# Experts' results scattered by rows to a table in DRAM and gathered per token, in place of a sorted buffer on the chip and a 0/1 matrix product

## The reference, cut to what matters

```python
oh_g = one_hot(top_k(x1 @ w_rg + b_rg, 1))            # group
le_sel = (x1 @ w_re + b_re)[group of the token]
e_val, e_idx = top_k(le_sel, 2)                        # two experts in it
comb = g_w * oh_g * (softmax(e_val) at e_idx)          # the two weights
y = sum over all 32 experts of ((silu(x1 @ w_gate) * (x1 @ w_up)) * comb) @ w_down
x2 = layer_norm(2 ** 0.25 * x1 + y)
gate = sigmoid(x2 @ w_ple_gate + b); x3 = layer_norm(2 ** 0.25 * x2 + gate * (p @ w_ple))
```

## Time and profile before

| what | us |
|---|---|
| median of three executions | 591.2 |
| span of the profiled execution | 587.8 |
| median less that span | 3.4 |
| TensorE busy in the span | 532.5 |
| VectorE busy | 291.9 |
| ScalarE busy | 193.0 |
| GpSimd busy | 58.6 |

### The profile page before, as it was taken

The page is one execution under the profiler, slowest core; times in us unless marked ns, Lnnn a source line. Parts: engine busy times, 40 slices in busy tenths (PEclk is TensorE's granted clock), DMA queues, the critical chain, the costliest instruction groups (busy, mean ns, idle before and its releaser), DMA issues.

```text
span 587.8 us, 9534 instructions
## 1 busy us (share of the span) xinstructions
PE 532.5 (91%) x3628; PEld 383.2 (65%) x3628; DVE 291.9 (50%) x621; ACT 193.0 (33%) x363; POOL 58.6 (10%) x86
## 2 busy tenths in 40 slices
PE   4999869999999979988999999998889899859992
PEld 3999768888999978756654545444444445346771
DVE  3442786565474865686722222312222222359976
ACT  4434443444462360163241111111111121345433
POOL 2000003322443420000000000000000000000121
PEclk9999999999999989979999999999999999969997
DMA  9995336865322940195739999999999999950001
GB/s 286 368 346 183 123 117 189 261 212 165 122 95 94 325 175 1 51 424 241 301 128 423 420 421 423 421 421 423 421 421 421 423 421 420 363 194 1 1 36 54
DMA packets 47563, 151.86 MB, mean 258 GB/s; under 512 B 3104, under 2 KB 27877, under 8 KB 35104
## 3 DMA queue, kind: packets, MB, share of 16 engines
q1 hardware_dynamic: 42754, 136.93, 60.2%
q0 software_dynamic: 3728, 12.08, 6.7%
q10 hardware_dynamic: 1046, 2.37, 1.2%
HBM read 148.59 MB, written 2.90 MB: 258 GB/s over the span
## 4 chain that ended last, share of the span: by engine, by line
PE 69%; DMA 12%; DVE 11%; ACT 4%; issue 3%; POOL 1%; SPq 0%; DVEq 0%; POOLq 0%; ACTq 0%
PE bank L1486 16%; PE bank L1805 15%; DMA ring<-in_w_up_dram 11%; PE bank L1454 8%; PE bank L1818 7%; PE bank L1674 5%; PE bank L1827 2%; PE bank L1904 2%; PE bank L1752 2%; PE bank L1432 1%; PE bank L1541 1%; ACT arena L630 1%; PE bank L1474 1%; PE bank L1811 1%; DMA arena<-in_x_prompt_dram 1%
## 5 line engine op out<-in xcount | busy, mean ns | idle before, releaser
L1805 PE MATMUL bank<-ring,arena 128*64 128x256 f32 x1024 | 128.9, 392 | 10.8 <-DMA ring<-in_w_up_dram 6.7
L1805 PEld LDWEIGHTS bank<-ring,arena 128*64 128x64 f32 x1024 | 70.9, 134 | 66.9 <-issue 27.5
L1243 DVE TENSOR_TENSOR arena<-bank,arena 128x512 f32 x32 | 22.1, 692 | 143.9 <-PE bank L1827 143.9
L1486 PE MATMUL bank<-x_high,w_high 128*128 128x320 f32 x248 | 79.1, 319 | 0.0
L1486 PE MATMUL bank<-x_low,w_high 128*128 128x320 f32 x248 | 76.6, 309 | 0.0
L1486 PE MATMUL bank<-x_high,w_low 128*128 128x320 f32 x248 | 76.4, 308 | 0.0
L1818 PE MATMUL bank<-ring,arena 128*64 128x512 f32 x256 | 61.9, 604 | 0.0
L895 DVE TENSOR_TENSOR w_low<-ring,w_high 128x1024 fp32r<-128x1024 f32 x32 | 40.0, 1258 | 29.7 <-ACT w_high L574 29.7
L1486 PEld LDWEIGHTS bank<-x_high,w_high 128*128 128x128 f32 x248 | 46.6, 188 | 1.4 <-issue 1.3
L1486 PEld LDWEIGHTS bank<-x_low,w_high 128*128 128x128 f32 x248 | 46.7, 188 | 0.1
L1486 PEld LDWEIGHTS bank<-x_high,w_low 128*128 128x128 f32 x248 | 46.5, 188 | 0.0
(11 more groups left out here) (301 smaller groups left out, 878.7 us busy)
## 6 DMA issues: line engine op xcount, KB each, us to landing
ring<-in_w_gate_dram SPq DMA_DIRECT2D x32, 1024.0 KB, 18.1
ring<-in_w_up_dram SPq DMA_DIRECT2D x32, 1024.0 KB, 20.1
ring<-in_w_down_dram SPq DMA_DIRECT2D x32, 1024.0 KB, 16.8
ring<-in_w_in_dram SPq DMA_DIRECT2D x16, 1024.0 KB, 10.2
arena<-in_cache_k_dram POOLq DMA_DIRECT2D x16, 256.0 KB, 4.4
arena<-in_cache_v_dram POOLq DMA_DIRECT2D x16, 256.0 KB, 3.2
ring<-in_w_o_dram SPq DMA_DIRECT2D x4, 1024.0 KB, 9.6
ring<-in_w_ple_gate_dram SPq DMA_DIRECT2D x4, 1024.0 KB, 15.6
```

The source lines that it names most:

```text
L1243: V.tensor_tensor(YsT[:, :, bass.ds(place, WIN)].rearrange("p (d c) n -> p c d n", d=2), b[:, :].rearrange("p (c d n) -> p c d n", c=4, d= ...
L1486: last = mm(bank[j % 2][:, 0:T], w[:, j % 4, k, :], x[:, k, :], start=(k == n == 0), stop=(k == KD - 1 and n == 2))
L1805: last = mm(b[WIN * f:WIN * (f + 1), 0:256].rearrange("p (s n) -> p s n", s=2), x[:, WIN * k:WIN * (k + 1)], w[:, :, k, f, :], start=(k == ...
```

## The change

The result of an expert is no longer turned and kept on the chip. ScalarE copies y into one of four `y_s` buffers in turn, and GpSimd issues an indirect DMA that writes its 128 rows of 512 numbers to `y_rows`, a table in DRAM of 1280 such rows, two for each pair, at row numbers that VectorE works out once (`result_rows`). Slots beyond the expert's count get a row number outside the table, and such rows are not written. When all 32 scatters have landed, GpSimd reads the flag, passes the loop for crowded experts and issues six indirect DMAs, which gather for each tile of tokens the first and the second row pair (4 KB a token) into `y_mine`. `combined` multiplies them by the token's two weights and adds them to x1, which VectorE has multiplied by 2 ** 0.25 after the first four experts. `turn_result`, `put`, `slot_weights`, `turn_pairs`, `pairs_out`, `turn_sorted` and `combine` go, with what belongs to them on ScalarE and VectorE. `high_gate` stands behind the last result now, all eight together; `low_gate` has four before and four after the first tile's norm. Loads of ln3 and the gate's bias wait for a semaphore that GpSimd raises once the gathers are issued. In `down`, TensorE now waits for ScalarE's copy of the result before.

```diff
@@ on-chip buffers
-        CT = at(69120, [P, PAIRS])
-        YsT = at(61440, [P, KD, SORTED])
+        y_s = [at(off, [P, 512]) for off in (69120, 71168, 73216, 85248)]
+        y_mine = at(38912, [P, 2 * TILES, D])
+        row_f = at(87296, [P, WINDOWS, 32])
-        x2 = at(61440, [P, TILES, D])
+        x2 = x1
+        y_rows = nc.dram_tensor("y_rows", (2 * PAIRS, 512), F32, kind="Internal").ap()
@@ GpSimd
+            def scatter(src, row, done):
+                pool.indirect_dma_start(y_rows, bass.IndirectOffsetOnAxis(ap=row, axis=0), src, None,
+                                        bounds_check=2 * PAIRS - 1, oob_is_err=False).then_inc(done, 16)
+            pool.wait_ge(rows_set, 1)
+            for n in range(EXPERTS):
+                pool.wait_ge(main["ys"], n + 1)
+                if n % 4 == 1 and n > 4:
+                    pool.wait_ge(y_out[3], 16 * (n // 4))
+                    pool.sem_inc(last_free, 1)
+                scatter(y_s[n % 4], row_i[:, 0, n:n + 1], y_out[n % 4])
+            for n in range(4):
+                pool.wait_ge(y_out[n], 16 * (EXPERTS // 4))
+            pool.wait_ge(starts_set, 1)
+            crowded = pool.value_load(flag[0:1, 0:1], min_val=0, max_val=1)
+            with pool.If(crowded > 0):
...
+            for t in ORDER:
+                r = ROWS[t]
+                for c in range(2):
+                    pool.indirect_dma_start(y_mine[0:r, 2 * t + c, :], None, y_rows.rearrange("(n d) f -> n (d f)", d=2),
+                                            bass.IndirectOffsetOnAxis(ap=mine_i[0:r, 3 * c + t:3 * c + t + 1], axis=0)).then_inc(y_here[t], 16)
+            pool.memset(scratch[:, 2:3], 0.0).then_inc(moe_done, 1)
@@ ScalarE
-            def result_out(q, n):
+            def result_out(q, n, b, free=None, turn=0):
                 act.wait_ge(q["y"], n)
-                nc.scalar.copy(y_s[:], bank[3][:, :]).then_inc(q["ys"], 1)
+                if free:
+                    act.wait_ge(free, turn)
+                nc.scalar.copy(y_s[b][:], bank[3][:, :]).then_inc(q["ys"], 1)
-                    pairs_out()
...
-            for g in range(10):
-                act.wait_ge(yt_ps, g + 1)
-                nc.scalar.copy(yj_high[:, g // 2, half_of(g)], bank[6 + g % 2][:, :]).then_inc(yt_a, 1)
...
+            for n in range(8):
+                high_gate(n)
@@ VectorE
+            def result_rows():
+                for w in range(WINDOWS):
+                    last = V.tensor_scalar(row_f[:, w, :], spare[:, :], float(WIN * w), ABSENT, ALU.is_le, ALU.mult)
+                link(last)
+                for w in range(WINDOWS):
+                    last = V.scalar_tensor_tensor(row_f[:, w, :], row_f[:, w, :], float(2 * WIN * w), base_f[:, :], ALU.add, ALU.add)
+                link(last)
+                V.tensor_copy(mine_i[:, :], places[:, :])
+                V.tensor_copy(row_i[:], row_f[:]).then_inc(rows_set, 1)
...
-                    before = place(first + (j - 2))
-                    put(main, first + (j - 1), bank[4 + (j + 1) % 2], before)
             first_experts()
+            for t in range(TILES):
+                v = x1[0:ROWS[t], t, :]
+                V.tensor_scalar(v, v, ALPHA, None, ALU.mult)
...
+            def combined(place):
+                t = ORDER[place]
+                r = slice(0, ROWS[t])
+                dve.wait_ge(y_here[t], 32)
+                v = x2[r, t, :]
+                link(V.scalar_tensor_tensor(v, y_mine[r, 2 * t, :], c1[r, t:t + 1], v, ALU.mult, ALU.add))
+                V.scalar_tensor_tensor(v, y_mine[r, 2 * t + 1, :], c2[r, t:t + 1], v, ALU.mult, ALU.add).then_inc(added, 1)
...
+            for n in range(4):
+                low_gate(n)
             dve.wait_ge(late_here, 32)
             combined(0)
+            norm2(0)
             combined(1)
-            norm2(0)
+            low_columns(0)
+            for n in range(4, 8):
+                low_gate(n)
+            norm2(1)
             combined(2)
@@ TensorE
             def down(q, n, slot):
                 pe.wait_ge(q["hT"], n)
+                if q is main and not (isinstance(n, int) and n == 1):
+                    pe.wait_ge(q["ys"], n + (-1))
...
-                    if behind[j] == 3:
+                    if behind[j] > 1:
                         other_half()
-                        turn_pairs()
-                    if behind[j] > 1:
-                        turn_result(main, first + (j - 2), bank[4 + j % 2])
...
-            turn_sorted(0)
-            for n in range(5):
-                if n < 4:
-                    turn_sorted(n + 1)
-                combine(n, 0)
...
+            turn_tile(x2, ORDER[0], x2t_ps, x2_set, 0)
```

More of the change, by code:

```diff
@@ L1261, in _ @@
             link(last)
-            for w in range(1, WINDOWS):
-                last = V.memset(start_f[:, w, 32:33], float(PAIRS))
-            link(last)
+            V.tensor_scalar(base_f[:, :], off, 2.0, cst[:, C_SLOT + 1:C_SLOT + 2], ALU.mult, ALU.add)
+            V.tensor_scalar(spare[:, :], bank[6][:, 160:192], cst[:, C_SLOT:C_SLOT + 1], None, ALU.subtract)
             link(V.tensor_reduce(cnt_max[:, 0:1], bank[6][:, 160:192], AX.X, ALU.max))
@@ L1781, in other_half @@
                     gather_all(j)
-            def turn_pairs():
-                pe.wait_ge(ga_out, 16)
-                for n in range(5):
-                    if n == 2:
-                        pe.wait_ge(ct_set, 1)
-                        for hf in range(2):
-                            mm(bank[6 + hf][:, 0:320], ones[:, :], CT[:, 320 * hf:320 * (hf + 1)], start=True, stop=True).then_inc(ct_set, 1)
-                    if n >= 2:
-                        pe.wait_ge(pj_set, n - 1)
-                    for t in range(TILES):
-                        r = ROWS[t]
-                        last = nc.tensor.transpose(bank[PAIR_BANKS[n]][:, P * t:P * t + r], PT[0:r, t, P * n:P * (n + 1)].bitcast(F32), ident[0:r, 0:r])
-                    last.then_inc(ga_ps, 1)
             def gate_up(q, slot, x, b, halfway=None):
@@ L1820, in down, with four_experts @@
                 last.then_inc(q["y"], 1)
-            def turn_result(q, n, b):
-                if isinstance(n, int) and n == 1:
-                    pe.wait_ge(pj_set, 5)
-                pe.wait_ge(q["ys"], n)
-                for c in range(4):
-                    last = nc.tensor.transpose(b[:, P * c:P * (c + 1)], y_s[:, P * c:P * (c + 1)], ident)
-                last.then_inc(q["yt"], 1)
-            def four_experts(first, slots, here, behind=(2, 2, 2, 2)):
+            def four_experts(first, slots, here, behind=(1, 1, 1, 1)):
                 for j in range(4):
@@ L1876, in _ @@
                     pe.wait_ge(over["w"], e * 48 + 48)
-                    for w in range(WINDOWS):
-                        n = e * WINDOWS + (w + 1)
+                    for w in range(1, WINDOWS):
+                        n = e * (WINDOWS - 1) + w
                         pe.wait_ge(over["xg"], n)
@@ L1882, in _ @@
                         down(over, n, 11)
[L1883 removed]
+                    pe.wait_ge(over["ys"], e * (WINDOWS - 1) + (WINDOWS - 1))
                     pe.sem_inc(over["freed"], 1)
[L1887 removed]
             pe.wait_ge(pe_out, 6)
[L1890 to L1918 removed]
+            turn_tile(x2, ORDER[0], x2t_ps, x2_set, 0)
             for j in range(6):
```

170 lines of the change are left out of this document (47 added, 123 removed).

## The result

The changed kernel takes 597.4 us (median; the kernel before 592.1 beside it): 1.0098 times as long, 95% interval 1.0051 to 1.0146. Run again later beside 29 executions of the kernel before (591.5), it took 598.3: 1.0108, 1.0051 to 1.0164. So it is 1% slower. The forecast was 587.3, 0.7% faster: the range of 580 to 603 over all rivals holds the time, the forecast's own range of 582 to 592 doesn't, and the direction was wrong. The profiled execution took 597.19 us, its span is 595.5.

A forecast was written before the change was run, and what follows sets the result against it. The weight stream was taken to bound the expert stretch, with a serial tail behind it. Gate job 1 starting 3.9 us earlier gave 587.8 - 3.9 = 583.9 of span, plus 3.4 around it 587.3 us; range 582 to 592, with rivals 580 to 603.

The forecast's parts named there:

- Start of the stream, 5.7 us: Start of the expert weight stream: turn_pairs and one turn_result leave the chain before expert 2's down, gaining 5.7 us.
- Middle, 8.6 us: Among the experts: scatters of 1280 written rows share the weights' DMA engines, losing 8.6 us at 108 ns a packet.
- rival C: Weight stream: rows crowd on a few DMA engines, slower, 592.5 or 606.3 us by case; chance 0.20.
- the low price of the three: Scatter traffic among the experts priced by bytes at 421 GB/s, 6.2 us; the other prices were 8.6 and 27.6.
- The last w_up lands one weight before the end of the stream, 502.6 - 2.5 = 500.1: End of the expert weights: last w_up lands at 500.1 before the shifts of -5.7 and +8.6 us.
- From the last w_up to the end of the last copy, 9.5: Last experts: gate and up, two down and the copies take 9.5 us, with no turn_result between.
- Tail: from the last result to the gathered rows, 13.8 us: After the experts: scatter landing, flag, jump, gather issue and landing sum to 13.8 us, bounds 7.6 and 23.2.
- From the gathered rows to job 1, 20.8: Tail: sums, norms, low columns, four low_gate and transposes take 20.8 us; gate job 1 starts at 547.1, not 550.96.
- What follows is as before: From gate job 1 to the end: unchanged from the kernel before, 36.8 us.
- D: Rival in the tail: GpSimd makes indirect DMAs slowly, three calls in series; 597.4 us at 4.5 us a call; chance 0.13.
- B: Rival: cheap scatters, 6.2 us, and a quick way back, 7.6 us in the tail's first part; 578.7 us; chance 0.27.
- the collision of GpSimd and VectorE: Tail: low_gate beside the last scatter's issue could cost up to 1.1 us, making the time 588.4.

The follow-up runs named there:

- the quiet run: Changed kernel with SyncE holding the last three gate weights and ln2 until all gathered rows landed; a measurement only, ending at 614 us.
- the kernel with all parts: Changed kernel with flag read early, short jump, tile 0's gathers first, all low_gate ahead of the wait, 25 constant matmuls: 588.7 us, 0.9955 of the kernel before.
- the fastest: The kernel with all parts, plus filled slots moved within their windows from the seventh expert on: 588.3 us, 0.9938 of the kernel before.
- the run with two gathers first: Changed kernel with GpSimd issuing tile 0's two gathers and waiting until both landed before the other four: 594.0 us.

## Why the prediction was wrong

**Start of the stream, 5.7 us: right.** 11.8 - 6.07 = 5.7.

**Middle, 8.6 us: right in sum, 8.7, wrong in make-up.** The price was taken as 108 ns for each written row, evenly. Dropped rows, which the choice left at nothing, cost some 1.4; uneven engines, rival C's mechanism, at least 1.6; what is left for the bytes of the written rows is at most 5.7, near the low price of the three and not the one chosen. How much of the 5.7 is unevenness too stays open. That the sum came out was luck.

**"The last w_up lands one weight before the end of the stream, 502.6 - 2.5 = 500.1": failed, 2.2 us.** Without scatters the last w_up is there 199.73 us after expert 2's `down` starts; from 302.63 that is 302.63 + 199.73 = 502.4, when TensorE took it up in the kernel before (502.54). The fall of GB/s after 502 was read as the stream's end; it was not. In the kernel before, the load of the last w_up was issued at 480.19 and landed 22.1 us later, at 502.3, that of the last w_down at 489.61 and 15.2 later, at 504.8. So the end was taken one weight too early, and the landing should have been asked of the queue. From the last w_up to the end of the last copy, 9.5, is right.

**"Tail: from the last result to the gathered rows, 13.8 us": failed, 5.8 us, the main miss.** By its terms: the scatter 6.06 for 4.4, and 0.77 for 0.1 before its issue begins; flag 0.83 for 0.6; the jump 3.43 for 2.57; issue 1.3 for 1.15; the gather 7.12 for 5.0. Every term was below, and the two landings most, by 1.7 and 2.1: each term was priced by the nearest single row, while on this path they stand in series under the worst neighbours, the gate weights with ln2 (3.7 us of the scatter, by the quiet run) and the gathers' own company (1.75 in this pair of profiles). The rows allowed it: 9.4 was the landing of a load behind others, and stood as the upper bound.

**From the gathered rows to job 1, 20.8: right (20.3).** The half clock of job 0 that the range allowed for was there: job 0 took 8.4 us.

**"What follows is as before": failed, 1.3 us.** VectorE's second half of low_gate, priced by the earlier trace rows up to job 1, isn't done with there: the norm behind it delays the sums of the next jobs. Moved ahead of the wait, the segment is 36.95, as before.

Forecast and measure differ by 2.2 + 5.8 + 1.3 - 0.5, which is 8.8 of the 8.9 us. D's mechanism, a slow call, is not it: an issue takes 0.98 us. That D's time at 4.5 us a call, 597.4, is the one measured is chance. B fell with the landings.

On the collision of GpSimd and VectorE: the 1.1 us that the prediction priced did not come. The last scatter's issue (518.22) began 0.2 us ahead of `low_gate` (518.42) and took 0.98. The gathers of the changed kernel are issued while VectorE waits; those of the kernel with all parts fall beside low_gate and the sums. The timeline of GpSimd, the second and third gather, first of the changed kernel, then of the fastest:

```profile
529.85 0.97 POOL L574 DMA_INDIRECT arena<-y_rows,small  x1 [0.30 <-issue]
531.12 0.92 POOL L574 DMA_INDIRECT arena<-y_rows,small  x1 [0.30 <-issue]
```

```profile
521.98 1.93 POOL L574 DMA_INDIRECT arena<-y_rows,small  x1 [0.30 <-issue]
527.50 1.92 POOL L574 DMA_INDIRECT arena<-y_rows,small  x1 [3.60 <-DMA arena<-y_rows,small]
```

Beside `low_gate` and the sums, both with two inputs in SBUF, the memory of `ring`, these issues take 0.95 to 1.0 us longer; not each one does, since the first gather of the fastest kernel, also beside `low_gate`, took 1.08. The Trainium skill (SBUF — State Buffer, "Who interferes with whom") says that a VectorE instruction with two inputs in SBUF contends with a GpSimd instruction that reads it. These rows fit that, for the issue of an indirect DMA too. It cost the tail little: from the start of the longer issue the second gather landed in 5.27 us, in the run with two gathers first, whose issue took 0.97, in 5.37; and tile 0 doesn't wait for the third gather. Of the four parts (3.24 for the jump, 1.75 for the gathers, 2.9 for `low_gate`, nothing for TensorE, together 7.9) 7.0 came, and where the other 0.9 went isn't shown.

What stays open: how much of the front's spread, 289.4 to 296.2, falls on either kernel on average; how the middle's loss divides between bytes and uneven engines; whether the distance of the jump alone makes its stall; and what a gather of 128 rows does in its 5.2 us alone.

## What to carry to other kernels

A result that goes through DRAM and back costs its landings in series, under the traffic of that moment: price each by the slowest comparable row, and ask which loads will be in flight just then. A matrix product that looks like pure overhead can be cheaper than the round trip, if it lies beside nothing better; and the wait that the trip opens should at once be filled with work that stands behind it (here low_gate, 2.9 us). A jump over much code that stands on the path may have to be paid for: here 3.4 us, and 0.85 with the code cut and the flag read earlier.

## What the runs showed of the hardware

- Rows of an indirect DMA that lie outside the table cost time: 28 scatters with none inside cost 2.07 us, 9.2 ns a row on a DMA engine on average (an estimate), and have 80 packets each, as many as those that write. The page's count of bytes written to HBM also takes them in: the kernel with 28 empty scatters has 13.91 MB, the kernel before 2.90; the difference is 2.62 for filling the table and 8.39, which is all 4096 rows of the 32 scatters, though the row of their queue shows 0.01 MB in 180 us of them.
- A scatter of 128 rows landed in 2.33 us alone (two profiles) and in 5.8 to 6.7 beside gate weights and ln2; a gather of as many, of twice the bytes, took 5.2 to 5.7 without other gathers and 6.3 to 7.1 with four behind it.
- GpSimd stalled for 3.2 to 3.4 us behind its jump past 128 rounds written out, and for 0.75 to 0.85 where one round or none was passed; the flag was read earlier there as well.
- GpSimd's issue of an indirect gather took 1.92 to 1.93 us in some places beside VectorE's two-input instructions, 0.91 to 1.00 while VectorE waited.
- The granted clock fell to 0.50 after a pause of 2.2 us, with 27 us of matmuls ahead of it; it stayed at 1.00 after a pause of 1.6 us with 52 or 72 us of matmuls ahead.
